# Convolution, output gate and key/value halves move beside the input projection, and half of the first output projection moves between attention steps

## The chip, the cores and the metric

The program runs on one core of a Trainium2 chip. The metric is the device time of one execution in microseconds (us), the median of several runs. Engines are named as in the profile: PE (TensorE), PEld (its weight loads), DVE (VectorE), ACT (ScalarE), POOL (GpSimd), SP (SyncE, which here only issues DMAs).

## What is computed

One layer of an encoder for 2,048 prompt tokens and 64 tokens of a running stream, all float32:

```python
gq, gk, gv, gr, glow, sq, sk, sv, cb, cc, ch = split_cols(x @ w_in)      # x is layer-normed
# A: gated linear attention, 4 heads, state carried over chunks of 64 tokens
lg = jax.nn.log_sigmoid(glow @ w_gate_up + b_gate) / GLA_TAU
S_fin, go = gla_seq(S0, gq * DK ** -0.5, gk, gv, lg)
go = go * lax.rsqrt(mean(go * go) + eps) * gla_norm_g * silu(gr)
# B: stick-breaking attention, 4 heads of 64, blocks of 128 queries, 512 cached keys for the stream
so = sb_attention(sq, k_all, v_all, past_len)
# C: short convolution of three taps over tokens
cy = conv3(cc * ch);  co = cb * cy
x = layer_norm(ALPHA * x + concatenate([go, so, co]) @ w_out)
x = layer_norm(ALPHA * x + square(relu(x @ w_up)) @ w_down)
```

The outputs are the two results, the new keys and values, the recurrent states and the last two rows of cc * ch.

## The kernel before

All matrix products of the layer are done as three passes over halves: an operand x is split into a rounded half (ACT copies it to fp32r, "hi") and a rest (DVE subtracts, "lo"), and `split_product` (L108 to L113) issues hi·hi, lo·hi, hi·lo. Three phases follow one another, each with its own buffers and a barrier at its end.

**phase_in** (L120) is the input projection. Tokens go in four groups (512, 512, 512 and 576). The columns of w_in go in six chunks of about 512; per group and chunk, PE runs four to eight units of 24 matmuls each. A written-out list `order` holds the steps norm (layer norm of one tile of 128 tokens), turn (its transposes, L357, and their halves), weights (halves of one chunk's eight row blocks) and product; every engine walks this one list. All four tiles of group 0 are normed and turned before the first product (L111 to L113). ACT evicts each unit and stores it: to `zt_scratch` transposed, to `gv_scratch`, or to the outputs of new keys and values.

**phase_gla** (L383) is the recurrence. Groups of 512 tokens, tiles of 128; again one list for all engines. For each group there is work ahead: gate, gate_log, gate_sum (decays, L701, L705), six levels of decayed products (level_arg L744 and L745, level_mul L754 and L760, level_product L859, level_put L790), and silu_exp and silu (three passes on ACT, L652 to L656, four on DVE, L732), which is spread between the steps of the tiles of the group before it. Per tile: v_in (load of values, L601), intra L903, inter L924, state L809, squares, root, turn, kv (L891) and norm (L820, L823), whose result store_tile (L566) puts into `mixt_scratch`. Beside all this POOL computes the convolution alone, in 10 pieces of at most 512 tokens (L948 to L983), from rows that phase_in stored.

**phase_tail** (L990) is attention, output projection and feed-forward. Attention is a list of 171 periods (one slot of scores z L1794 to L1796, sigmoids L1544 and L1545, scan L1671, product L1681 or on POOL L1715, turn L1808, weigh L1821 and L1822); 20 of them belong to the first 512 tokens. Keys and values are read back from the outputs in six pieces, transposed and split (pk L1782, L1522, L1642; pv; p_store L1435 and L1437 to `ks_scratch` and `vs_scratch`) and these steps stand between the first 20 periods. Then come rows, xn, mix_load (L1417), mix (halves of the eight row blocks of the mixed values: 0 to 3 from A, 4 and 5 from B, 6 and 7 from C), and the output projection: for the first group 16 steps `out` of 12 matmuls, eight on blocks 0 to 3 (kh = 0) and eight on 4 to 7 (kh = 1). Feed-forward steps up and down follow, and the other 151 periods are spread over them by `price` and `cost`, so that each group's attention is there before its output projection. SP issues all loads and stores of the tail in the same order, and a wait on SP holds back whatever stands behind it.

## Time and profile before

| | |
|---|---|
| median of 3 runs | 3114.15 us (3110.86 to 3116.0) |
| the profiled execution | 3112.73 us, of which the span is 3110.9 us |
| phase_in, to 640.9 us | first product at 42.3 us, last at 637.3 us |
| phase_gla | 640.9 to 959.7 us |
| phase_tail | from 959.7 us, first `out` at 1110.5 us |
| busy over the span | PE 88%, DVE 48%, ACT 34%, POOL 11% |
| mean granted clock of PE | 0.934 |

A busy time is the sum of an engine's instructions in a stretch; matmuls overlap, so their durations add up to more than their stretch, and what one costs in a row of them is the distance of two starts.

### The profile page before, as it was taken

The page shows a single profiled execution, that of the slowest core. Times are in us where ns is not written, and L with a number is a line of the kernel's source. Part 1 is how long each engine was busy: PE and PEld are TensorE (multiplying, and loading weights), DVE is VectorE, ACT ScalarE, POOL GpSimd, SP SyncE. Part 2 cuts the span into 40 slices and gives each one's busy share as a digit, 9 for nine tenths or more (in the row PEclk, how much of TensorE's full clock was granted, in tenths as well). Part 3 has the DMA queues.
Part 4 walks back from the last instruction along what each step waited for, and adds up shares of the span by engine and source line. Part 5 has one row for each costly group of instructions (what it writes and reads, how often), then busy time and mean ns, then how long its engine had stood idle before and what let it go on. Part 6 is the DMA issues. An engine that isn't in the chain of part 4 may idle for free. (4 is left out here: it accounts for less than half of the span.)

```text
span 3110.9 us, 38667 instructions
## 1 busy us (share of the span) xinstructions
PE 2734.4 (88%) x13838; PEld 2268.3 (73%) x13838; DVE 1505.1 (48%) x2247; ACT 1069.5 (34%) x1783; POOL 329.9 (11%) x283
## 2 busy tenths in 40 slices
PE   5999999946662467999998999999999988999997
PEld 4787789835541356888877888877888766888885
DVE  5333342158883556665656544446644425522224
ACT  3323333223342424443443444443434321322221
POOL 1100010056600000000001100001100000000000
PEclk9999999966786588999999999999999989999998
DMA  5544454233315654575655766565766554544452
GB/s 185 169 160 153 160 180 126 85 121 88 89 45 187 191 191 140 169 249 179 216 193 191 229 218 209 191 206 183 234 190 227 170 171 144 190 157 158 154 168 98
DMA packets 362107, 526.11 MB, mean 169 GB/s; under 512 B 28832, under 2 KB 208208, under 8 KB 361920
## 3 DMA queue, kind: packets, MB, share of 16 engines
q1 hardware_dynamic: 337696, 480.23, 48.1%
q10 hardware_dynamic: 18832, 26.10, 2.3%
q0 software_dynamic: 5392, 17.31, 1.6%
q8 instruction: 115, 1.88, 0.3%
q14 instruction: 72, 0.59, 0.1%
HBM read 422.74 MB, written 100.80 MB: 168 GB/s over the span
## 5 line engine op out<-in xcount | busy, mean ns | idle before, releaser
L111 PE MATMUL p_ps_u<-p_xh,p_wh 128*128 128x512 f32 (+1 forms) x1280 | 453.1, 354 | 5.4 <-DVE p_xl L1626 5.4
L112 PE MATMUL p_ps_u<-p_xh,p_wl 128*128 128x512 f32 (+1 forms) x1280 | 451.5, 353 | 0.0
L113 PE MATMUL p_ps_u<-p_xl,p_wh 128*128 128x512 f32 (+1 forms) x1280 | 451.0, 352 | 0.0
L1575 DVE SCALAR_TENSOR_TENSOR p_res<-p_res,p_ps_d 128x512 f32<-128x512 f32 (+1 forms) x340 | 232.1, 685 | 451.4 <-PE p_ps_d L113 445.7
L111 PE MATMUL p_ps_d<-p_wh,p_hh 128*128 128x512 f32 (+1 forms) x1088 | 433.2, 398 | 16.9 <-DVE p_res L1575 14.8
L112 PE MATMUL p_ps_d<-p_wh,p_hl 128*128 128x512 f32 (+1 forms) x1088 | 428.6, 394 | 0.0
L113 PE MATMUL p_ps_d<-p_wl,p_hh 128*128 128x512 f32 (+1 forms) x1088 | 428.4, 394 | 0.0
L1484 ACT ACTIVATE p_wh<-p_wst 128x1024 fp32r<-128x1024 f32 x288 | 293.9, 1049 | 276.6 <-PE p_ps_d L113 225.0
L1633 DVE TENSOR_TENSOR p_r<-p_r 128x512 f32<-128x512 f32 (+1 forms) x160 | 95.8, 599 | 461.3 <-ACT p_hh L1514 461.3
L1507 ACT ACTIVATE p_r<-p_ps_u 128x512 f32<-128x512 f32 (+1 forms) x160 | 83.8, 524 | 579.5 <-PE p_ps_u L113 579.4
L111 PEld LDWEIGHTS p_ps_u<-p_xh,p_wh 128*128 128x128 f32 x1280 | 241.2, 188 | 35.5 <-DVE p_xl L1626 6.2
L113 PEld LDWEIGHTS p_ps_u<-p_xl,p_wh 128*128 128x128 f32 x1280 | 241.2, 188 | 31.0
L112 PEld LDWEIGHTS p_ps_u<-p_xh,p_wl 128*128 128x128 f32 x1280 | 241.2, 188 | 28.3
L111 PEld LDWEIGHTS p_ps_d<-p_wh,p_hh 128*128 128x128 f32 (+1 forms) x1088 | 204.0, 187 | 66.4 <-DVE p_res L1575 19.1
L111 PE MATMUL p_ps_m<-p_xh,p_wh 128*128 128x512 f32 (+3 forms) x680 | 242.4, 356 | 1.4 <-DVE p_xl L320 1.4
L112 PE MATMUL p_ps_m<-p_xh,p_wl 128*128 128x512 f32 (+3 forms) x680 | 242.9, 357 | 0.0
L113 PE MATMUL p_ps_m<-p_xl,p_wh 128*128 128x512 f32 (+3 forms) x680 | 241.2, 355 | 0.0
L113 PEld LDWEIGHTS p_ps_d<-p_wl,p_hh 128*128 128x128 f32 (+1 forms) x1088 | 203.4, 187 | 48.3
L329 DVE TENSOR_TENSOR p_wl<-p_wst,p_wh 128x512 fp32r<-128x512 f32 (+1 forms) x192 | 127.6, 703 | 224.6 <-ACT p_wh L272 224.4
L112 PEld LDWEIGHTS p_ps_d<-p_wh,p_hl 128*128 128x128 f32 (+1 forms) x1088 | 204.1, 188 | 44.0
L1715 POOL TENSOR_TENSOR p_aw<-p_sg,p_keep 128x512 f32<-128x512 f32 (+2 forms) x84 | 89.9, 1070 | 1363.3 <-DVE p_keep L1671 1363.3
L1544 ACT ACTIVATE p_tg<-p_ps_z 128x512 f32<-128x512 f32 (+5 forms) x168 | 87.4, 520 | 323.1 <-PE p_ps_z L1796 322.9
(155 smaller groups left out, 4473.0 us busy)
## 6 DMA issues: line engine op xcount, KB each, us to landing
p_wl<-wlo_scratch SPq DMA_DIRECT2D x216, 512.0 KB, 5.1
p_wst<-in_w_up SPq DMA_DIRECT2D x128, 512.0 KB, 6.0
p_wst<-in_w_down SPq DMA_DIRECT2D x128, 512.0 KB, 4.6
wlo_scratch<-p_wl SPq DMA_DIRECT2D x72, 512.0 KB, 3.6
p_wst<-in_w_in SPq DMA_DIRECT2D x128, 256.0 KB, 3.6
p_kk<-ks_scratch SPq DMA_DIRECT2D x84, 256.0 KB, 5.9
p_vv<-vs_scratch SPq DMA_DIRECT2D x84, 256.0 KB, 4.5
p_wst<-in_w_out SPq DMA_DIRECT2D x32, 512.0 KB, 6.0
```

What stands on the lines that cost most here:

```text
L111: pe.matmul(out, lhs_hi, rhs_hi, start=first, stop=False, skip_group_check=skip)
L112: pe.matmul(out, lhs_lo, rhs_hi, start=False, stop=False, skip_group_check=skip)
L113: return pe.matmul(out, lhs_hi, rhs_lo, start=False, stop=last, skip_group_check=skip)
L329: dve.tensor_tensor(wl[:, gc % 2, k, :width], wst[:, u % WSTAGE, :width], wh[:, gc % 2, k, :width].bitcast(F32), ALU.subtract).then_inc(wl ...
L1484: act.activation(wh[:, u % WRING, :], wst[:, u % WSTG, :], ACT.Copy).then_inc(whi_done, 1)
L1507: act.activation(r[:, i % 2, :cc], ps_u[:, i % 2, :cc], ACT.Relu).then_inc(relu_done, 1)
L1544: act.activation(tg[:m, n % SIG, 512 - w:512], ps_z[:m, :w], ACT.Sigmoid, scale=-SCALE).then_inc(sig_done, 1)
L1575: dve.scalar_tensor_tensor(out=acc, in0=acc, scalar=scale, in1=ps_d[:c, d % DB, :], op0=ALU.mult, op1=ALU.add).then_inc(d_free, 1)
L1633: dve.tensor_tensor(r[:, i % 2, :cc], r[:, i % 2, :cc], r[:, i % 2, :cc], ALU.mult).then_inc(sq_done, 1)
L1715: pool.tensor_tensor(aw[:m, u % AW, i, :w], sg[:m, n % SIG, :w], keep[:m, n % KEEP, 513 - w:513], ALU.mult).then_inc(a_pool, 1)
```

## The change

In phase_in the list is written out unit by unit: a product waits only for its own tile where it can, the chunk gv comes first, weights are split three blocks per unit, and the layer norm takes its root on POOL. Units get kinds: `silu` (ACT applies a sigmoid while evicting, DVE multiplies by the value and the norm's weight), `cc`/`ch`/`cb` (DVE does the convolution and stores into `mixt_scratch`), and `kv`, whose values are split at once and whose keys are transposed (kturn) and split, straight into `ks_scratch` and `vs_scratch`. phase_gla loses silu_exp, silu and all of POOL's convolution; it loads the finished gate instead. phase_tail prepares only the cached keys and values. Blocks 6 and 7 of the mixed values are split before 4 and 5; those two are loaded after the eight `out` steps with kh = 0, and in the first group these eight steps stand between the first 20 periods.

```diff
@@ phase_in
+    chunks = [([(C_GV, 512)], "T"), ([(C_GQ, 512)], "F"), ([(C_GR, 528)], "F"), ([(C_SK, 512)], "T"), ([(C_CC, 512)], "F"),
+              ([(C_SQ, 256), (C_CB, 256)], "F")]
...
+                        order += [("norm_b", x + 1)] * (x + 1 < len(us)) + [("turn", x)]
+                    order += [("norm_a", x + 2)] * (x + 2 < len(us))
...
+                order += more[3 * x:3 * x + 3]
+                order.append(("unit", i))
+                order += late.pop(0)
...
+                if units[i]["kind"] == "kv":
+                    late[0].append(("kturn", i))
+                    late[1].append(("kstore", i))
...
+                        act.activation(slot[:u["mw"], :u["n"]], ps[:u["mw"], :u["n"]], ACT.Sigmoid if kind == "silu" else ACT.Copy).then_inc(a_out, 1)
...
+                            dve.tensor_tensor(cu[:, x, at_u + 2:at_u + 2 + n], ps[:, c:c + n], cin[:, c:c + n], ALU.mult).then_inc(d_out, 1)
...
+                            dve.tensor_scalar(y, cu[:, x, at_u + 2:at_u + 2 + n], cw[:, x, 2:3], None, ALU.mult).then_inc(conv_step, 1)
+                            for w in range(2):
...
+                                dve.scalar_tensor_tensor(out=y, in0=cu[:, x, at_u + w:at_u + w + n], scalar=cw[:, x, w:w + 1], in1=y,
+                                                         op0=ALU.mult, op1=ALU.add).then_inc(conv_step, 1)
...
+                    for p in range(2):
+                        mm = pe.transpose(ps_t[:, q, p * P:p * P + n], outb[:n, slot_no[i] % OUTS, p * P:p * P + P], ident[:n, :n])
+                    mm.then_inc(k_turned, 1)
...
+                        if i == by_chunk[gc][0]:
+                            pe.wait_ge(wlo_done, KT * gc + k + 1)
@@ phase_gla
-                if li == 0:
-                    todo.append((("silu_exp", g), 0))
-                elif li == 2:
-                    todo.append((("silu", g), 3))
...
-                    if g >= 1:
-                        sp.wait_ge(gg_done, g)
-                    sp.dma_start(gr[:, :, :n], zt_dram[Z_GR:Z_GR + 512, t0:t0 + n].rearrange("(a p) t -> p a t", p=P)).then_inc(gr_in, 16)
+                    if g >= 2:
+                        sp.wait_ge(o_gate, tiles_before[g - 1])
+                    sp.dma_start(gg[:, sl_, :, :n], zt_dram[Z_GR:Z_GR + 512, t0:t0 + n].rearrange("(a p) t -> p a t", p=P)).then_inc(gg_in[sl_], 16)
...
-            for k, (x, t, n) in enumerate(pieces):
...
-                pool.dma_start(mixt_dram[768 + cp:768 + cp + P, t:t + n], y).then_inc(c_out[sl_], 16)
@@ phase_tail
-            steps = [("mix", g, k) for k in range(KT)]
+            steps = [("mix", g, k) for k in (0, 1, 2, 3, 6, 7)]
             for kh in range(2):
+                if kh:
+                    steps += [("mix_load", g, 4), ("mix_load", g, 5), ("mix", g, 4), ("mix", g, 5)]
...
-        mixed = [i for i, st in enumerate(dense) if st[0] == "mix" and st[2] == 0]
+        mixed = [i for i, st in enumerate(dense) if st[0] == "mix_load" and st[2] == 4]
...
+        order += [("q_load", 0), ("k_load", 0), ("q_prep", 0)]
+        add_attention(1)
+        order += [("w_load", 0), ("w_load", 1), ("p_load",)]
+        add_attention(2)
+        split_weights(-1)
...
+            if i < mixed[0]:
+                if st[0] == "out":
+                    seen += 1
+                    order += prep[seen // 2 - 1:seen // 2] if seen % 2 == 0 else []
+                    add_attention(2 + (group_end[0] - 2) * seen // (firsts + 1))
+                continue
```

The lists move instructions in three places that matter below. First, SP's queue in phase_gla near the third tile of group 0: p_gr (now p_gg) is the gate, p_on a tile's result, p_v the values of the tile after next. Before:

```order
L594 DMA p_gr<-zt_scratch 128x4x512 [waits p2_gg_done]
L566 DMA mixt_scratch<-p_on 128x4x128 [waits p2_o_gate]
L601 DMA p_v<-gv_scratch 128x512 [waits p2_o_mm]
L566 DMA mixt_scratch<-p_on 128x4x128 [waits p2_o_gate]
L601 DMA p_v<-gv_scratch 128x512 [waits p2_o_mm]
```

Now:

```order
L780 DMA p_gg<-zt_scratch 128x4x512 [waits p2_o_gate]
L755 DMA mixt_scratch<-p_on 128x4x128 [waits p2_o_gate]
L787 DMA p_v<-gv_scratch 128x512 [waits p2_o_mm]
L755 DMA mixt_scratch<-p_on 128x4x128 [waits p2_o_gate]
L787 DMA p_v<-gv_scratch 128x512 [waits p2_o_mm]
```

The sequence is the same, but the first load, with a result's store and the values' load behind it, now waits for o_gate, the results of all four tiles of the group, where it waited for gg_done.

Second, PE at the start of the tail, where p_ps_z are scores, p_ps_d an `out` step and p_ps_a transposes (L1885 those of the cached keys, L1911 of weights). Before:

```order
L1782 MATMUL p_ps_a<-p_ident,p_res 128x128 x12
L1794 MATMUL p_ps_z<-p_causalb,p_identb 128x128
L1795 MATMUL p_ps_z<-p_kk,p_qh 128x128
L1796 MATMUL p_ps_z<-p_kk,p_ql 128x128
L1782 MATMUL p_ps_a<-p_ident,p_res 128x128 x4
L1794 MATMUL p_ps_z<-p_causalb,p_identb 128x128
```

Now (of each `out` step's 12 matmuls the last three stand here):

```order
L1899 MATMUL p_ps_z<-p_kk,p_ql 128x256
...
L111 MATMUL p_ps_d<-p_wh,p_xh 128x512
L112 MATMUL p_ps_d<-p_wh,p_xl 128x512
L113 MATMUL p_ps_d<-p_wl,p_xh 128x512
L1897 MATMUL p_ps_z<-p_causalb,p_identb 128x128
L1898 MATMUL p_ps_z<-p_kk,p_qh 128x128
L1899 MATMUL p_ps_z<-p_kk,p_ql 128x128
L1897 MATMUL p_ps_z<-p_causalb,p_identb 128x128
L1898 MATMUL p_ps_z<-p_kk,p_qh 128x256
L1899 MATMUL p_ps_z<-p_kk,p_ql 128x256
L1911 MATMUL p_ps_a<-p_ident,p_aw 128x128 x3
L111 MATMUL p_ps_d<-p_wh,p_xh 128x512
```

After the first two periods one `out` step stands before every two further periods.

Third, DVE's queue at the start of phase_in: L451 are weight rests, L435 and L438 the norm of a tile, L417 to L426 its statistics, L445 the rests of a turned tile. Now:

```order
L445 TENSOR_TENSOR p_xl<-p_ps_t,p_xh 128x4x128 x2
L451 TENSOR_TENSOR p_wl<-p_wst,p_wh 128x512
L454 TENSOR_SCALAR p_gn<-p_gn 128x4
L451 TENSOR_TENSOR p_wl<-p_wst,p_wh 128x512 x7
L435 SCALAR_TENSOR_TENSOR p_xn<-p_xs,p_mv,p_g_b 128x1024
L438 SCALAR_TENSOR_TENSOR p_xn<-p_xn,p_rstd,p_b_b 128x1024
...
L451 TENSOR_TENSOR p_wl<-p_wst,p_wh 128x512 x3
L435 SCALAR_TENSOR_TENSOR p_xn<-p_xs,p_mv,p_g_b 128x1024
L438 SCALAR_TENSOR_TENSOR p_xn<-p_xn,p_rstd,p_b_b 128x1024
L445 TENSOR_TENSOR p_xl<-p_ps_t,p_xh 128x4x128 x2
```

Tile 1 is turned behind tile 2's norm and three weight rests of the next chunk; before, all four tiles stood ahead of the first product.

## Rows read from the trace of the kernel before

**Rows 1.** Windows of the whole core by stage; columns are in its first row

```profile
core 0: us, PE busy (x) PEld busy (x) DVE busy (x) ACT busy (x) POOL busy (x), PEclk, DMA share, GB/s
...
42.30:637.60 595.30, 595.27 (x2960) 493.11 (x2960) 182.88 (x288) 185.90 (x340) 38.45 (x26) 1.00 0.45 146
640.90:725.90 85.00, 37.46 (x154) 28.72 (x154) 59.33 (x63) 20.86 (x19) 63.10 (x51) 0.55 0.34 114
725.90:788.90 63.00, 40.53 (x278) 31.91 (x277) 55.40 (x85) 26.93 (x32) 37.05 (x38) 0.80 0.36 93
788.90:859.40 70.50, 42.51 (x277) 34.40 (x276) 60.39 (x85) 26.93 (x32) 37.22 (x38) 0.76 0.38 98
859.40:920.00 60.60, 38.10 (x293) 31.13 (x292) 52.44 (x88) 27.80 (x36) 0.00 (x0) 0.83 0.17 43
959.70:1110.50 150.80, 47.26 (x191) 36.92 (x191) 65.27 (x101) 53.95 (x112) 9.14 (x11) 0.52 0.69 221
1110.50:1136.00 25.50, 25.46 (x113) 20.83 (x114) 11.99 (x18) 6.42 (x12) 0.64 (x1) 0.94 0.41 131
...
1230.00:3060.00 1830.00, 1773.32 (x8902) 1485.23 (x8900) 875.43 (x1262) 656.44 (x1081) 113.42 (x93) 0.99 0.59 191
```

**Rows 2.** Timeline of TensorE, first products: start us, duration us, instruction [idle before]

```profile
42.29 0.79 PE L111 MATMUL p_ps_m<-p_xh,p_wh 128*128 128x512 f32 x1 [1.41 <-DVE p_xl L320]
```

**Rows 3.** Timeline of TensorE, one tile's eight transposes in mid-projection

```profile
96.10 1.04 PE L357 MATMUL p_ps_t<-p_ident,p_xn 128*128 128x128 f32 x8
```

**Rows 4.** Groups by form, 641 to 957 us: busy us, mean ns | idle before

```profile
L760 DVE TENSOR_TENSOR p_qb<-p_ex,p_gq 64x512 f32<-64x512 f32 x48 | 42.0, 874 | 0.8
...
L732 DVE SCALAR_TENSOR_TENSOR p_gg<-p_gr,p_gn,p_gg 128x512 f32<-128x512 f32 x16 | 12.6, 846 | 0.0
```

**Rows 5.** The first of these groups from 850 to 900 us, with GpSimd idle

```profile
L760 DVE TENSOR_TENSOR p_qb<-p_ex,p_gq 64x512 f32<-64x512 f32 x9 | 6.1, 683 | 0.1
```

**Rows 6.** The same view from 671 to 716 us, GpSimd busy

```profile
L760 DVE TENSOR_TENSOR p_qb<-p_ex,p_gq 64x512 f32<-64x512 f32 x12 | 15.7, 1306 | 0.2
```

**Rows 7.** Timeline of all engines around the end of the recurrence's first group

```profile
775.55 0.50 SPq L601 DMA_DIRECT2D p_v<-gv_scratch  x1
...
785.27 0.68 PE L891 MATMUL p_ps_s<-p_v,p_kt 64*64 64x128 f32 x16
...
785.88 1.12 PE L839 MATMUL p_ps_g<-p_glow,p_wgu 16*128 16x512 f32 x2
...
786.79 1.50 DVE L823 TENSOR_TENSOR p_on<-p_on,p_gg 128x512 f32<-128x512 f32 x1
...
792.98 1.23 DVE L701 SCALAR_TENSOR_TENSOR p_gy<-p_gy,p_ga 128x1024 f32<-128x1024 f32 x1 [4.18 <-ACT p_ga L635]
```

**Rows 8.** DMA issues, 640 to 957 us: KB each, median us to landing

```profile
p_v<-gv_scratch SPq DMA_DIRECT2D x16, 256.0 KB, 3.6
```

**Rows 9.** Timeline of SP's queue at the start of the tail

```profile
959.72 0.35 SPq L1360 DMA_DIRECT2D p_ident<-in_ident  x1
...
1002.57 0.38 SPq L1378 DMA_DIRECT2D p_wst<-in_w_out  x1
...
1012.87 0.38 SPq L1378 DMA_DIRECT2D p_wst<-in_w_out  x1
...
1094.60 0.46 SPq L106 DMA_DIRECT2D p_g_b<-in_ln_g  x1
```

**Rows 10.** Timeline of TensorE, first product of the output projection and two later

```profile
1110.54 0.80 PE L111 MATMUL p_ps_d<-p_wh,p_xh 128*128 128x512 f32 x1 [19.71 <-DVE p_xl L1607]
...
1134.09 0.39 PE L111 MATMUL p_ps_d<-p_wh,p_xh 128*128 128x512 f32 x1
1134.32 0.39 PE L112 MATMUL p_ps_d<-p_wh,p_xl 128*128 128x512 f32 x1
```

**Rows 11.** Timeline of TensorE, scores of two attention steps

```profile
1083.56 0.56 PE L1795 MATMUL p_ps_z<-p_kk,p_qh 128*128 128x256 f32 x1
...
1088.66 0.71 PE L1795 MATMUL p_ps_z<-p_kk,p_qh 128*128 128x512 f32 x1
```

754 lines of the change are left out of this document (415 added, 339 removed).

## The prediction, made before the change was run

> **What bounds the kernel now.** I read the windows by stage first, for the share of each engine in each stage, then the timelines where stages begin and end, then the groups of the recurrence by form. In the windows, PE is busy for all of the 595.3 us behind the first product of phase_in, while DVE works 183 us and ACT 186 [rows 1]. So that phase is PE's, and only its first 42.3 us, in which no product runs, can be shortened [rows 2]. In phase_gla DVE leads: 59.3 of the 85 us of the work ahead, 55.4 of 63 in group 0, 60.4 of 70.5 in group 1; there POOL computes the convolution. In group 2 POOL is idle, and DVE needs 52.4 us for the same kind of group [rows 1]. In the tail, 150.8 us pass before the first `out`, and PE is busy for 47.3 of them at a mean granted clock of 0.52, which is nearly all the lower level, 1.2 GHz. From 1230 to 3060 us it is busy for 97% at 0.99, 2.4 GHz. PE's chain sets the end: time moved out of the waiting stretches is gained, work added in the full stretches is paid.
>
> **phase_in.** The first product waits for a DVE rest (its idle names p_xl) and comes at 42.29 us because four tiles are normed and turned ahead of it. Now it needs one tile. Group 0's first chunk is four units of 24 matmuls, 96 at a pitch of 0.23 us [rows 10], 22 us, plus some 2.5 for the first at half clock (0.79 against 0.39 us) [rows 2, 10]: it ended near 66.8 us. In the new list the later units of the chunk wait for DVE, which has per tile a norm, two rests and three weight rests in front: some 7.5 us, an estimate from DVE operations of 0.7 to 1.5 us of like form [rows 4, 7]. With the first product near 15 us and the fourth tile near 50, the second chunk begins at about 57: a gain of 9.8. What is added to PE: the new keys are transposed here, 34 pairs of 128 x 128 at 0.13 us each transpose (1.04 for eight) [rows 3], half of them in place of idle PE time at the start and group changes, so 34 x 0.13 = 4.4 us. The convolution, gate product, halves of values and keys lie on DVE and ACT, whose busy share of 31% covers them; if that cover failed, PE would wait at units for a PSUM buffer. Sum **-5 us**, ends 0 (each unit waits as DVE comes) and -12.
>
> **phase_gla.** Three of the four constants of the convolution and its loads no longer stand at the start: 1.5 us, taken as a tenth of the idle there. While POOL works, DVE's decayed products take 1306 ns instead of 683 [rows 5, 6]: 12 x 0.62 = 7.5 us in the work ahead. The other DVE operations of that stage I take at 4 more, an estimate from the mean of the whole phase, 874 against 683 [rows 4, 5]. In groups 0 and 1 DVE is busy 3.0 and 8.0 us longer than in group 2 [rows 1]; less the part of it that is `silu` I take 9.5. The `silu` passes themselves, 16 of 0.85 us, are 12.6 [rows 4] with 0.9 of overhead. Together -36 us.
>
> Against it stands a new wait. SP now issues the load of a group's gate only when o_gate shows that all four tiles of the group two before it have been normed and gated. Behind it stand a result's store and p_v, the values of a tile that the next group needs. Before, the p_v that group 1 starts with was issued at 775.55; the last result of group 0 was gated from 786.79, for 1.50 us [rows 7]. So p_v would be issued no sooner than about 789.2 and, with 3.6 us to land [rows 8], be there at 792.8, where kv (L891) used it at 785.27 [rows 7]: 7.6 us late. DVE, the bound of this stage, goes on meanwhile with work ahead, but the list lets it do only what stands before the tile's own steps (it idled 4.18 us at 792.98 once before, for ACT). Two crossings at 7.6 and a third, shorter one at 6 make +21 us. What is behind the wait: on SP stores and loads, on PE the state's product and all of the next tile. Between -36 (the wait is hidden, as the values of that tile are due later) and 0 (a late p_v moves the work ahead too) I take **-15 us**.
>
> **phase_tail.** The stage before the first `out` held, on SP, one pair of weight units per 10 us (1002.57, 1012.87), and the normed rows only at 1094.60; 15.9 us later came the first `out` [rows 9, 10]. In the new list two attention periods and two pairs are ahead of the rows. From the start at 959.7, 6 us for constants and two pairs at 10 bring the rows to 986, with 15.9 and one more to 1003. Only what is new relative to this start counts. Then 18 periods and eight `out` steps alternate. Two starts of scores two periods apart are 5.1 us apart [rows 11], and an `out` of 12 matmuls costs 12 x 0.23 = 2.7 us at full clock [rows 10]. PE waits within the periods, so part of it is covered: I take 7.0 us for a round of two periods and one `out`, between 5.1 and 7.8. Nine rounds are 63 us, the first `out` at half clock adds 2.7, the cached keys' preparation between them 8: 1077 us. Then the attention's result is stored, blocks 4 and 5 are loaded and split: twice 3.6 us [rows 8] and 2 of halves. kh = 1 starts near 1087. Before, it started eight `out` steps behind 1110.54, at 1135 to 1136 (113 matmuls run there in 25.5 us) [rows 1, 10]: -48 us. More attention is now left behind that point (by my count of the list, 20 periods lie before it, where 22 did), which costs some PE time in the full stretch: two to three slots of about 1.2 us, +3. In later groups blocks 4 and 5 are loaded in the middle of a group, beside dense work; one wait moves, none is added, 0 with ends at 3 either way. Sum **-45 us**, ends -22 (rounds of 9 us, one more load in line) and -60 (rounds of 5.3).
>
> The clock weighs here. The row shows 0.52 in the stretch in which PE works in pieces of one to two us between waits, and 0.94 as soon as `out` steps run without a break [rows 1]. My sum uses full clock for all but the first. The Trainium skill ("TensorE: Matmul & The Clock Gate", section "HAM oscillation — how this bites in real kernels") says that short bursts of matmuls between waits make each burst start at the lower clock again. This case's 0.52 agrees with that for attention steps; no row shows it for an `out` between them. By that rule the result would be the one of the third case below.
>
> **Sum.** -5 - 15 - 45 = -65 us. The profiled execution took 3112.73, so 3047.7; the median of the runs is 1.4 above it, so **3049 us**.
>
> **The rivals, and how the numbers follow.**
>
> *As summed*, 3049 us: 0.50.
>
> *The late values are hidden.* For: the v_in behind the gate may be of a tile whose state step comes late, and DVE has work ahead to fill with; against: kv at 785.27 stands 2 us before the end of the group. Then phase_gla gives its -36, and if the periods also run at the pace of 5.3 us a round, 31 us in all: 3018 us. 0.25.
>
> *The `out` steps between attention run at half clock.* For: 0.52 in the same stretch. Against: one `out` adds 2.7 us of dense work to each round. At half clock it costs 5.4 instead of 2.7: seven more at 2.7 us are 19: 3068 us. 0.18.
>
> *Slower than before.* The change holds the rows' order to attention: every `out` waits in PE's queue behind periods that wait for ACT and DVE, and these in turn wait behind it. In the kernel before, the 20 periods with their preparation took from 988 to about 1090, 102 us, 10.2 for two. If that pace, and not 5.1 us, is attention's own, a round costs 10.2 + 5.4 at half clock + 1 of preparation, 16.6 us, and nine of them 150. kh = 1 then starts at 1003 + 150 + 9 = 1162, 26 us later than before, and with the displaced periods the tail is 29 longer: 29 - 5 - 15 = +9, 3122 us. The mechanism decides from a round of about 15.6 us. Against: most of that pace came from loading keys (pairs of loads at 10 us), which the change removes. 0.04.
>
> *Nothing to measure.* The halved load of the convolution's stage does not shorten it and the tail's gain is lost again at the next group's end: 0.03.
>
> A measurement of this kernel can tell about 0.2%, 6 us, from no change. Faster: 0.50 + 0.25 + 0.18 = 0.93, same 0.03, slower 0.04. The range reaches below the second case by 10 us, 3008, since phase_in's end of -12 and the tail's of -60 can add to it, and above the third by 24, 3092, for phase_gla's end of 0.
>
> **What would show it.** Right: first product near 15 us and the second chunk near 57, last product of phase_in near 632 to 636; DVE's decayed products at about 690 ns throughout and POOL idle in phase_gla; phase_gla about 304 us long, with waits of kv on DMA p_v near the ends of groups; first `out` about 43 us behind the start of the tail, kh = 1 about 127 behind it; scores two periods apart at 7 us. Wrong: a DVE or ACT wait inside phase_in's units, which lets PE's busy share fall below 97%; no wait on p_v (then the second case); a granted clock of 0.5 in the alternating stretch (the third); rounds above 10 us (the fourth). I would also be wrong if attention, now two periods later, missed the end of the second group, seen as waits of PE for mix_load 4 in the later groups.

## The result, and the profile after

The changed kernel took 3084.11 us in the median of four runs (3081.57 to 3086.94), the kernel before 3113.14 in the runs beside it: a ratio of 0.9907, interval 0.9889 to 0.9924. It is faster, by 29 us where 65 were forecast. The profiled execution took 3083.57 us, its span is 3081.8.

Four points that both programs have split the span: the last product of phase_in, the first load of the tail (`p_ident`), the first product of kh = 1 of the first group, and the end. In the kernel before they lie at 637.28, 959.72, 1135.45 and 3110.9 us; two of them are these products, and its second chunk of phase_in begins at 68.23:

```profile
68.23 0.48 PE L111 MATMUL p_ps_m<-p_xh,p_wh 128*128 128x512 f32 x1
...
637.28 0.29 PE L113 MATMUL p_ps_m<-p_xl,p_wh 128*128 128x288 f32 x1
...
1135.45 0.39 PE L111 MATMUL p_ps_d<-p_wh,p_xh 128*128 128x512 f32 x1
```

| stretch | before | after | difference | forecast |
|---|---|---|---|---|
| phase_in to its last product | 637.3 | 638.3 | +1.0 | -5 |
| from there to the tail | 322.4 | 319.8 | -2.6 | -15 |
| tail to kh = 1 | 175.7 | 122.1 | -53.6 | -48 |
| kh = 1 to the end | 1975.5 | 2001.5 | +26.0 | +3 |

The windows of the changed kernel, columns as in [rows 1]:

```profile
core 0: us, PE busy (x) PEld busy (x) DVE busy (x) ACT busy (x) POOL busy (x), PEclk, DMA share, GB/s
15.60:62.30 46.70, 31.46 (x120) 24.22 (x121) 28.26 (x41) 12.59 (x23) 4.95 (x7) 0.82 0.56 181
62.30:638.60 576.30, 574.88 (x2899) 475.85 (x2897) 240.93 (x409) 179.88 (x350) 20.29 (x28) 1.00 0.48 152
642.00:708.90 66.90, 29.68 (x154) 21.79 (x154) 44.49 (x58) 15.36 (x16) 6.10 (x2) 0.67 0.25 84
708.90:779.40 70.50, 41.09 (x277) 31.96 (x276) 49.41 (x81) 21.32 (x29) 0.00 (x0) 0.77 0.20 61
779.40:851.30 71.90, 41.91 (x277) 32.55 (x276) 49.28 (x81) 21.32 (x29) 0.00 (x0) 0.78 0.20 59
851.30:917.10 65.80, 38.89 (x277) 32.45 (x276) 49.30 (x81) 20.94 (x29) 0.00 (x0) 0.81 0.13 37
958.10:1000.80 42.70, 1.53 (x7) 1.10 (x7) 9.79 (x15) 10.36 (x17) 0.76 (x2) 0.50 0.80 274
1000.80:1080.20 79.40, 50.21 (x247) 40.44 (x247) 48.70 (x75) 34.25 (x77) 8.85 (x9) 0.80 0.47 146
1005.00:1035.00 30.00, 24.23 (x133) 19.40 (x132) 25.28 (x40) 16.38 (x39) 4.21 (x5) 0.99 0.38 116
1080.20:3080.00 1999.80, 1884.42 (x9395) 1573.71 (x9395) 972.94 (x1399) 694.89 (x1153) 131.36 (x108) 0.97 0.57 183
```

In phase_in PE is busy for 31.5 of the first 46.7 us behind the first product, then it is full. The work ahead of phase_gla lasts 66.9 us instead of 85.0, and POOL has two instructions left in it and none in the groups; but groups 0, 1 and 2 last 70.5, 71.9 and 65.8 us, where [rows 1] has 63.0, 70.5 and 60.6 (one group up to 920), with DVE busy for only some 49.3 in each. In the tail the alternating stretch has full clock (0.99 from 1005 to 1035; 0.80 is the mean from the first `out` to kh = 1). The first products of each part, on PE's timeline:

```profile
15.63 0.76 PE L111 MATMUL p_ps_m<-p_wh,p_xh 128*128 128x512 f32 x1 [2.10 <-DVE p_wl L451]
...
37.51 0.79 PE L111 MATMUL p_ps_m<-p_wh,p_xh 128*128 128x512 f32 x1 [9.18 <-DVE p_xl L445]
...
1000.77 0.79 PE L111 MATMUL p_ps_d<-p_wh,p_xh 128*128 128x512 f32 x1 [34.54 <-DVE p_xl L1714]
...
1080.27 0.76 PE L111 MATMUL p_ps_d<-p_wh,p_xh 128*128 128x512 f32 x1 [9.44 <-issue]
...
1565.89 0.47 PE L111 MATMUL p_ps_d<-p_wh,p_xh 128*128 128x512 f32 x1 [2.03 <-issue]
...
2054.25 0.77 PE L111 MATMUL p_ps_d<-p_wh,p_xh 128*128 128x512 f32 x1 [7.05 <-issue]
...
2569.00 0.76 PE L111 MATMUL p_ps_d<-p_wh,p_xh 128*128 128x512 f32 x1 [7.40 <-issue]
```

37.51 is the second unit of phase_in, late by 9.18 us. The last four are the first products of kh = 1 in groups 0 to 3. Each stands behind a wait, and the kernel before has none of the four: there the products of kh = 1 followed those of kh = 0 with nothing between. ACT's timeline names what the last of them waits for, the load of blocks 4 and 5:

```profile
2566.68 1.43 ACT L1603 ACTIVATE p_xh<-p_hh 128x576 fp32r<-128x576 f32 x2 [4.82 <-DMA p_hh<-mixt_scratch]
```

DVE's decayed products take 682 ns throughout, as forecast (874 in [rows 4]):

```profile
L923 DVE TENSOR_TENSOR p_qb<-p_ex,p_gq 64x512 f32<-64x512 f32 x48 | 32.7, 682 | 0.8
```

Why the groups gain nothing by it stands on SP's queue at the end of group 0:

```profile
744.48 0.47 SPq L777 DMA_DIRECT2D p_gk<-zt_scratch  x1
765.94 0.36 SPq L780 DMA_DIRECT2D p_gg<-zt_scratch  x1
766.35 0.51 SPq L755 DMA_DIRECT2D mixt_scratch<-p_on  x1
766.90 0.50 SPq L787 DMA_DIRECT2D p_v<-gv_scratch  x1
```

and on PE's timeline there:

```profile
773.45 1.15 PE L1055 MATMUL p_ps_s<-p_v,p_kt 64*64 64x128 f32 x16 [9.66 <-DMA p_v<-gv_scratch]
774.52 2.07 PE L1003 MATMUL p_ps_g<-p_glow,p_wgu 16*128 16x512 f32 x2
...
779.43 2.08 PE L1067 MATMUL p_ps_o<-p_att,p_v 128*128 128x128 f32 x8
```

SP stands for 21 us at p_gg. The store and the load of p_v behind it go out at 766.35 and 766.90, and kv waits 9.66 us for the values. The same happens twice more, 9.53 us at 845.34 and 6.70 at 914.31.

### The profile page after: what moved, and what is told of

The parts are those of the page before. It is cut to its first block and busy times, and to the rows that moved or that the text cites. A ratio compares the mean times of both kernels' runs of the same rounds, so it can differ in the third digit from the quotient of the medians.

```text
span 3081.8 us, 38633 instructions
## 1 busy us (share of the span) xinstructions
PE 2721.1 (88%) x13838; PEld 2254.1 (73%) x13838; DVE 1521.8 (49%) x2339; ACT 1027.9 (33%) x1758; POOL 178.2 (6%) x169
## 5 line engine op out<-in xcount | busy, mean ns | idle before, releaser
L451 DVE TENSOR_TENSOR p_wl<-p_wst,p_wh 128x512 fp32r<-128x512 f32 (+1 forms) x192 | 123.9, 689 | 135.7 <-ACT p_wh L348 134.7
L111 PE MATMUL p_ps_d<-p_wh,p_xh 128*128 128x512 f32 (+1 forms) x272 | 115.2, 424 | 78.1 <-issue 43.6
```

The lines of the kernel that those rows point to most:

```text
L111: pe.matmul(out, lhs_hi, rhs_hi, start=first, stop=False, skip_group_check=skip)
L451: dve.tensor_tensor(wl[:, gc % 2, k, :width], wst[:, w % WSTAGE, :width], wh[:, gc % 2, k, :width].bitcast(F32), ALU.subtract).then_inc(wl ...
```

## The experiments

Fifteen kernels ran. Each is the changed kernel with the edit shown; none leaves out any work. "From kh = 1" means from the first product of kh = 1 of group 0 to the end of the profiled execution. One profile scatters: phase_gla takes 319.4 to 328.3 us, from the last product to the tail, in the kernels whose edit doesn't touch it, and the stretch from kh = 1 takes 2000.7 to 2004.6 in the six kernels that have the change's tail. A difference below that is not read from one profile, so the 2.6 us by which phase_gla is shorter than before are none. Steadier is the rest of phase_in behind the first product of its second chunk: 575.0 to 575.2 us wherever that part is left alone. Times are medians; the interval of a ratio is some 5 us wide to either side, so two medians 6 us apart are not told apart.

### The wait for o_gate

**g1_gate_late.** The gate's load is issued at the last tile's store:

```diff
-                    if g >= 2:
-                        sp.wait_ge(o_gate, tiles_before[g - 1])
-                    sp.dma_start(gg[:, sl_, :, :n], zt_dram[Z_GR:Z_GR + 512, t0:t0 + n].rearrange("(a p) t -> p a t", p=P)).then_inc(gg_in[sl_], 16)
+                    if g < 2:
+                        sp.dma_start(gg[:, sl_, :, :n], zt_dram[Z_GR:Z_GR + 512, t0:t0 + n].rearrange("(a p) t -> p a t", p=P)).then_inc(gg_in[sl_], 16)
...
                 elif it[0] == "norm":
                     store_tile(sp, it[1])
+                    g = tiles[it[1]][0]
+                    if it[1] == group_tiles[g][-1] and g + 2 < NG:
+                        t0, n = GG[g + 2]
+                        sp.dma_start(gg[:, g % 2, :, :n], zt_dram[Z_GR:Z_GR + 512, t0:t0 + n].rearrange("(a p) t -> p a t", p=P)).then_inc(gg_in[g % 2], 16)
```

> The changed kernel, with one move in phase_gla: the load of a group's gate into the buffer of two groups before is issued behind the store of that group's last tile, so that its wait on o_gate holds nothing back on SP. Theory (SP's wait on o_gate is what ate the gain of phase_gla): the three waits of kv on p_v (9.66, 9.53 and 6.70 us of PE's idle time) go, groups 0, 1 and 2 last about 60 us instead of 70.5, 71.9 and 65.8, and the phase shortens from 316 to 286-294 us; the time falls to 3054-3062 us. Rival (the crossings are set by the gate chain, for which DVE idles 7.7 to 8.3 us at gate_sum, and the values only come late beside it): p_v is early, but DVE idles as long at gate_sum, the phase shortens by less than 8 us, the time stays above 3075 us.

Measured: 3055.02 us, ratio 0.9816 (0.9801 to 0.9831), 29 us less than the change. PE's timeline at the same crossing:

```profile
766.07 0.68 PE L1058 MATMUL p_ps_s<-p_v,p_kt 64*64 64x128 f32 x16
766.68 1.12 PE L1006 MATMUL p_ps_g<-p_glow,p_wgu 16*128 16x512 f32 x2
...
769.69 1.90 PE L1070 MATMUL p_ps_o<-p_att,p_v 128*128 128x128 f32 x8
```

kv starts without a wait, and the next tile 3.6 us behind it instead of 6.0 (779.43 - 773.45), since the gate products between them (L1003 and L1006 of the two kernels) take 1.12 us and not 2.07: behind the wait they run at the lower clock. Groups 0 to 2 last 61.1, 61.2 and 58.0 us, the tail begins at 928.9 instead of 958.15, and from the last product of phase_in to it pass 291.0 us instead of 319.8 (289.7 to 291.7 in the three kernels below that have this edit too). The theory holds. DVE's waits for the gate's chain, of which the rival spoke, fell with it, from 40.9 to 32.5 us in all: in part they hung on the late kv.

### The start of phase_in

**i1_turn_first**

```diff
-                        order += [("norm_b", x + 1)] * (x + 1 < len(us)) + [("turn", x)]
+                        order += [("turn", x)] + [("norm_b", x + 1)] * (x + 1 < len(us))
```

> The changed kernel, but in the first chunk of phase_in a tile is turned ahead of the norm of the next one, not behind it. Theory (DVE's queue sets the start: the second unit waited 9.18 us for rests that stand behind three weight rests and the next tile's norm, some 7 us): the second unit starts near 31 instead of 37.5 us, and the second chunk 4 to 7 us earlier than 62.3; the time falls by 4 to 7 us. Rival (the arrival of weights and ACT's halves set it, for which DVE waits 0.7 to 1.9 us at each rest): the first chunk ends within 2 us of 62.3 all the same, since the later units wait for their tiles instead; no change beyond 3 us.

Measured: 3086.67 us, ratio 0.9917 (0.9897 to 0.9938); the second unit starts at 34.49, the second chunk at 62.71 (37.51 and 63.14 in the change). The rival holds. ACT's timeline names the wait:

```profile
28.39 0.63 ACT L348 ACTIVATE p_wh<-p_wst 128x512 fp32r<-128x512 f32 x1 [6.18 <-DMA p_wst<-in_w_in]
29.80 0.63 ACT L348 ACTIVATE p_wh<-p_wst 128x512 fp32r<-128x512 f32 x1 [0.78 <-DMA p_wst<-in_w_in]
31.51 0.63 ACT L348 ACTIVATE p_wh<-p_wst 128x512 fp32r<-128x512 f32 x1 [1.08 <-DMA p_wst<-in_w_in]
32.04 0.58 ACT L368 ACTIVATE p_outb<-p_ps_m 128x512 f32<-128x512 f32 x1
32.52 1.08 ACT L340 ACTIVATE p_xh<-p_ps_t 128x512 fp32r<-128x512 f32 x2
```

ACT waits for three weight loads, then evicts the first unit, and only then makes the turned tile's halves (p_xh, 32.52).

**i2_weights_later** is i1 and this, to remove that:

```diff
-                order += more[3 * x:3 * x + 3]
+                order += more[3 * x:3 * x + 3] if gc else []
                 order.append(("unit", i))
                 order += late.pop(0)
+                order += more[3 * x - 3:3 * x] if not gc and x else []
```

> The changed kernel, but in the first chunk of phase_in a tile is turned ahead of the next tile's norm, and the weights of the second chunk are split only behind the units 1, 2 and 3 (three, three, two blocks), none behind unit 0. In the run that changed the first of these alone, ACT waited 6.2 us for a weight load before each group of three halves, with the turned tile's halves behind it. Theory (ACT's and DVE's queues hold the turned tile behind weights whose loads have not landed): the second unit starts at 28 to 31 us instead of 37.5, the second chunk begins at 53 to 58 instead of 62.3 us, last product of phase_in 4 to 8 us earlier; the time falls by 4 to 8 us. Rival (the second chunk then waits for its own weights, which come one in 1.3 to 2 us): the second chunk's first unit stalls between its row blocks for what was gained, and the last product stays within 2 us of 638.6.

Measured: 3092.85 us, ratio 0.9937 (0.9922 to 0.9951), 9 us worse than the change, last product at 644.08. The second unit does start at 28.78, but the next two start at 39.82 and 51.56, and the second chunk at 66.98:

```profile
34.65 0.60 ACT L369 ACTIVATE p_outb<-p_ps_m 128x512 f32<-128x512 f32 x1 [6.91 <-PE p_ps_m L113]
...
35.14 1.14 ACT L349 ACTIVATE p_wh<-p_wst 128x512 fp32r<-128x512 f32 x2
37.21 0.63 ACT L349 ACTIVATE p_wh<-p_wst 128x512 fp32r<-128x512 f32 x1 [0.93 <-DMA p_wst<-in_w_in]
37.74 1.07 ACT L341 ACTIVATE p_xh<-p_ps_t 128x512 fp32r<-128x512 f32 x2
```

Behind a unit ACT now has its eviction (waited for 6.91 us), the weights and the next tile in a row, so that units no longer overlap with the halves of the next. The theory fell, and the rival's last product within 2 us of 638.6 did too.

**i3_norms_first** restores the old start:

```diff
-        order = [("x_load", 0), ("consts",), ("x_load", 1), ("norm_a", 0), ("norm_b", 0), ("norm_a", 1), ("turn", 0)]
-        order += [("w", 0, k) for k in range(KT)] + [("x_load", 2), ("norm_b", 1), ("x_load", 3)]
+        order = [("x_load", 0), ("consts",), ("x_load", 1), ("norm_a", 0), ("norm_b", 0), ("norm_a", 1)]
+        order += [("w", 0, k) for k in range(KT)] + [("norm_b", 1), ("turn", 0), ("x_load", 2), ("norm_a", 2), ("norm_b", 2), ("turn", 1)]
+        order += [("x_load", 3), ("norm_a", 3), ("norm_b", 3), ("turn", 2), ("turn", 3)]
...
-                    if x:
-                        order += [("norm_b", x + 1)] * (x + 1 < len(us)) + [("turn", x)]
-                    order += [("norm_a", x + 2)] * (x + 2 < len(us))
```

> The changed kernel, but in phase_in all four tiles of the first group are normed and turned ahead of the first product, as in the kernel before (units, kinds and everything behind the first chunk are those of the change). This undoes the start alone. Theory (the new start ends the first chunk at 62.3 instead of some 67 us, a gain of 5, and no more, since ACT waits for weights' loads with the turned tile's halves behind them): first product at 38 to 43 us, the second chunk from 64 to 68 us, last product of phase_in 2 to 6 us later than 638.3; time 3086-3090 us. Rival (the new start is worth the 9.8 us that were forecast, and something else in the phase took 5 of them): last product 8 us or more later, 3092 us or above.

Measured: 3085.0 us, ratio 0.9917 (0.9897 to 0.9936): no difference (its profiled execution is the longest, 3094.73, with the longest phase_gla of all). PE's timeline:

```profile
38.42 0.78 PE L111 MATMUL p_ps_m<-p_wh,p_xh 128*128 128x512 f32 x1
...
62.38 0.48 PE L111 MATMUL p_ps_m<-p_xh,p_wh 128*128 128x512 f32 x1
```

First product 22.8 us later than in the change, second chunk 0.8 us earlier, last product 637.46. Both expectations missed: the interleaved start is worth nothing. The 5 us that the first chunk ends earlier than before come from the rest of the start, which both have (first product at 38.42 with the old order, 42.29 before; which of its parts does it was not tried).

**i4_kturn_twice** does PE's transposes of new keys twice:

```diff
-                    for p in range(2):
+                    for p in (0, 1, 0, 1):
```

> The changed kernel, but PE does each transpose of new keys twice, into the same place (34 transposes of 128 x 128 more, no other engine does more). Theory (PE bounds phase_in behind the first product, and a transpose costs it its full 0.13 us): last product of phase_in 4 to 5 us later, time 3087-3090 us. Rival (they fall into PE's gaps, and the 5.9 us that the phase is longer behind its first chunk are something else): last product within 1 us of 638.3.

Measured: 3088.7 us, ratio 0.9929 (0.9912 to 0.9945), last product at 641.56. The phase behind the first chunk takes 578.1 us instead of 575.2: 2.9 us for 34 transposes more, 0.09 each. They are on the path. The 0.13 of the forecast was the duration of eight by eight; eight in a row hold the next product back by 0.79 us (67.44 to 68.23 in the kernel before), 0.10 each. One pair in the change:

```profile
137.74 0.38 PE L567 MATMUL p_ps_t<-p_ident,p_outb 128*128 128x128 f32 x2
137.88 0.48 PE L111 MATMUL p_ps_m<-p_xh,p_wh 128*128 128x512 f32 x1
138.19 0.39 PE L112 MATMUL p_ps_m<-p_xh,p_wl 128*128 128x512 f32 x1
```

From the pair's start to the product behind it pass 0.14 us (0.36 with the pair done twice), and from that product to the next 0.31 instead of 0.23, in both kernels. So a pair costs 0.22 us, of which doubling shows only the part of the transposes, and 17 pairs cost 3.7. Behind its first chunk the phase is 6.1 us longer than before (638.31 - 63.14 against 637.28 - 68.23). Besides the pairs, three transposes of new tiles wait for DVE's norm, 1.4 us in all, where none did before; the last us is open.

### The tail up to kh = 1

**u1_attention_first** takes the first group's attention out from between the `out` steps, and issues the load of blocks 4 and 5, in every group, ahead of the last of those with kh = 0 (in groups 1 to 3 this is the edit of m2 below):

```diff
             elif st[0] == "mix":
+                if st == ("mix", 0, 0):
+                    add_attention(group_end[0])
...
+                    order += prep[seen:seen + 1]
                     seen += 1
-                    order += prep[seen // 2 - 1:seen // 2] if seen % 2 == 0 else []
-                    add_attention(2 + (group_end[0] - 2) * seen // (firsts + 1))
...
                 if kh:
-                    steps += [("mix_load", g, 4), ("mix_load", g, 5), ("mix", g, 4), ("mix", g, 5)]
+                    steps += [("mix", g, 4), ("mix", g, 5)]
                 for h in range(2):
+                    if h and not kh:
+                        steps += [("mix_load", g, 4), ("mix_load", g, 5)]
```

> The changed kernel, but the first group's attention is not spread between its out steps: all 20 periods stand ahead of the first halves of the mixed values, the eight out steps of kh = 0 follow in one row with the cached keys' preparation between them, and blocks 4 and 5 are loaded ahead of the last four out steps in every group. Theory (the gain of the tail up to kh = 1 came from spreading: the out steps fill PE's waits for ACT and DVE): without it kh = 1 starts 10 to 20 us later than at 1080.3, the time is 3090-3100 us. Rival (it came from what is no longer done there, the preparation of new keys and the convolution's blocks, and from the earlier load of rows; PE's time is not what bounds this stretch): kh = 1 starts within 5 us of 1080.3 or earlier, the time is 3075-3086 us.

Measured: 3078.45 us, ratio 0.9894 (0.9878 to 0.9911), 6 us less than the change, as m2 alone (3078.37).

```profile
1050.99 0.79 PE L111 MATMUL p_ps_d<-p_wh,p_xh 128*128 128x512 f32 x1 [5.05 <-DVE p_xl L1717]
...
1078.63 0.75 PE L111 MATMUL p_ps_d<-p_wh,p_xh 128*128 128x512 f32 x1 [2.03 <-issue]
```

The first `out` comes 50 us later than in the change, kh = 1 1.6 us earlier, and the tail itself begins 1.9 earlier (956.28): from its start to kh = 1 pass 122.4 us, against 122.1. The rival holds: the 54 us do not come from spreading. One reserve: the early load shortens the wait ahead of kh = 1 from 9.44 to 2.03 us here, so up to 7 us of spreading's worth may hide in it. By exclusion the rest comes from what both orders share: no new keys and values are loaded, transposed and split there, and the rows are normed early. This is argued, not shown; it was not divided further.

**t1_periods_first** does six more periods in the wait for the mixed values:

```diff
+                if st == ("mix", 0, 0):
+                    add_attention(8)
-                    add_attention(2 + (group_end[0] - 2) * seen // (firsts + 1))
+                    add_attention(8 + (group_end[0] - 8) * seen // (firsts + 1))
```

> The changed kernel, but six more attention periods of the first group (eight instead of two) stand ahead of the first halves of the mixed values, in the 34.5 us in which PE waits for rows and mixed values; the other twelve are spread over the eight out steps as before. Nothing else moves: the same 20 periods precede kh = 1. Theory (between 964 and 1001 us PE only waits for loads, and each period moved there gives back the 2.5 to 3 us it takes beside the out steps): the first out comes at most 5 us later, kh = 1 starts 10 to 18 us earlier than 122 us behind the start of the tail, and the whole gain reaches the end: 3066-3075 us. Rival (the wait is not PE's alone: the loads of keys and values put ahead hold back rows and weights on SP, and ACT and DVE make the halves later by what the periods take): the first out comes 10 us or more later, and the time stays within 4 us of 3084.

Measured: 3082.58 us, ratio 0.9903 (0.9888 to 0.9918). First `out` 12.8 us later, kh = 1 7.0 us earlier (1073.24), and the stretch from there 2008.9 us, 7.4 longer than in the change: what was won ahead of kh = 1 was lost behind it, and nothing is clear in the time. ACT shows what the periods waited for:

```profile
1001.23 0.42 ACT L1643 ACTIVATE p_qh<-p_qraw 128x256 fp32r<-128x256 f32 x1 [17.92 <-DMA p_qraw<-zt_scratch]
```

The third head's queries came 17.9 us late: they stand on SP behind rows and mixed values, were issued from 990.16, and the slowest load of queries took 10.3 us to land where the median took 3.0. The window 958 to 1000.8 above has 274 GB/s and a DMA share of 0.80, and t1 from 958.7 to 1001.2 has 297 and 0.88. The opening of the tail is a stretch of loads, and PE's 34.5 us of idle are no free room.

**t2_periods_more** is t1 with four periods of the second group ahead of kh = 1, two of them behind the load of blocks 4 and 5 (its diff is against t1):

```diff
-        begun, spent = group_end[0], 0.0
+        begun, spent = group_end[0] + 4, 0.0
...
+                if st == ("mix_load", 0, 5):
+                    add_attention(group_end[0] + 4)
...
-                    add_attention(8 + (group_end[0] - 8) * seen // (firsts + 1))
+                    add_attention(8 + (group_end[0] + 2 - 8) * seen // (firsts + 1))
```

> As the run with eight periods first, and four periods of the second group are done ahead of kh = 1 too, two of them over the load of blocks 4 and 5. Theory (part of what the tail gave back is attention displaced into the full stretch: a period costs about 2.5 us there, PE's passes for it and the clock and waits around it, and next to nothing in a wait): kh = 1 starts 2 to 6 us later than with the eight periods alone, the stretch behind it is 9 to 12 us shorter, the time is 4 to 9 us below that run's. Rival (the stretch behind kh = 1 is not shortened by fewer periods, since its end is set by waits at the group changes): the time is that of the other run or a few us above it.

Measured: 3100.83 us, ratio 0.9958 (0.9941 to 0.9975), 18 us worse than with eight periods alone. kh = 1 starts at 1100.84, 27.6 us later, of which 4.8 lie ahead of the tail; from kh = 1 it takes 2003.0 us, 5.9 less than t1 where 9 to 12 were expected, and no less than the change. The theory fell: four periods cost over 20 us here and give back 6 at most.

### From kh = 1 to the end

**m1_mix_first** puts blocks 4 and 5 of groups 1 to 3 ahead of the first `out`, as before the change:

```diff
-                if kh:
+                if kh == (0 if g else 1):
                     steps += [("mix_load", g, 4), ("mix_load", g, 5), ("mix", g, 4), ("mix", g, 5)]
```

> The changed kernel, but in groups 1 to 3 blocks 4 and 5 are loaded and split ahead of the first out step, as in the kernel before; group 0 keeps the new order. Theory (the tail gave back 27 of its 54 us mostly by a new wait ahead of kh = 1 in each later group: 2.03, 7.05 and 7.40 us of idle and some 2 us of lower clock behind each of the two long ones): these waits go, the waits ahead of the first out step stay at 5 to 7 us as in the kernel before, and the time falls by 15 to 22 us to 3062-3069. Rival (the time was given back by attention that was displaced from the first group into the full stretch): the time stays within 5 us of 3084 and the wait turns up ahead of the first out step instead.

Measured: 3081.48 us, ratio 0.9901 (0.9886 to 0.9916), from kh = 1 1999.9 us. The waits ahead of kh = 1 are gone in these groups, but in the first group's feed-forward six scores waited for q rests, 11.2 us together, where one did in the kernel before (1.9) and three in the change (5.7). This is one of them:

```profile
1493.29 0.29 PE L1897 MATMUL p_ps_z<-p_causalb,p_identb 128*128 128x128 bf16 x1 [2.60 <-DVE p_ql L1760]
```

**m2_mix_early** issues only the two loads earlier in these groups, ahead of the last `out` steps of kh = 0:

```diff
-                    steps += [("mix_load", g, 4), ("mix_load", g, 5), ("mix", g, 4), ("mix", g, 5)]
+                    steps += [] if g else [("mix_load", g, 4), ("mix_load", g, 5)]
+                    steps += [("mix", g, 4), ("mix", g, 5)]
                 for h in range(2):
+                    if g and h and not kh:
+                        steps += [("mix_load", g, 4), ("mix_load", g, 5)]
```

> The changed kernel, but in groups 1 to 3 the two loads of blocks 4 and 5 are issued ahead of the last four or five out steps of kh = 0 and split behind them, so that 11 us of products lie over the load. Theory (the wait ahead of kh = 1 is the round trip of load and halves with nothing in its place): no idle over 1.5 us ahead of kh = 1 in any of these groups, 3062-3070 us, about as fast as with both blocks first. Rival (attention of the group is late, and the loads wait for its result): the wait moves with the load, the idle ahead of kh = 1 stays at 5 us or more and the time falls by less than 6 us.

Measured: 3078.37 us, ratio 0.9887 (0.9865 to 0.9909), from kh = 1 1997.4 us. The waits ahead of kh = 1 shrink to 2.0 to 2.2 us, 10 us less together; the time hardly follows. Both theories of a single cause had failed by here.

**m3_old_plan** is m1 and the counts of attention periods of the kernel before:

```diff
+        first_out = [i for i, st in enumerate(dense) if st[0] == "out"][0]
-        price = [0.0 if i in quiet or i < mixed[0] or i >= mixed[-1] else cost.get(st[0], 0.0) * (st[1] if st[0] == "pause" else 1) for i, st in enumerate(dense)]
+        price = [0.0 if i in quiet or i < first_out or i >= mixed[-1] else cost.get(st[0], 0.0) * (st[1] if st[0] == "pause" else 1) for i, st in enumerate(dense)]
...
                     add_attention(2 + (group_end[0] - 2) * seen // (firsts + 1))
+                spent += price[i]
                 continue
```

> The changed kernel with blocks 4 and 5 ahead of the first out step in groups 1 to 3, and with the attention of everything behind kh = 1 of the first group planned as in the kernel before: 22 periods precede that point instead of 20 (the last two over the load of blocks 4 and 5), and the counts of periods in front of each up, down and out step behind it are those of before. Theory (what the tail gave back was the order of the later groups: waits ahead of kh = 1, and, in the run that only moved the two blocks, attention planned at other places, whose q rests came 2.2 to 2.6 us late six times): from kh = 1 to the end it takes 1976 to 1985 us, as before (1975.5), instead of 2001.5; kh = 1 itself starts 3 to 7 us later than at 1080.3; time 3060-3070 us. Rival (the give-back lies in something the change does to the later groups whatever their order, such as a lower clock or longer waits behind an earlier start): from kh = 1 to the end 1995 us or more, time 3080 us or above.

Measured: 3067.05 us, ratio 0.9848 (0.9833 to 0.9862), 17 us less than the change. The theory holds. **m4_plan_only** has this diff without that of m1.

> The changed kernel with only the plan of the run m3_old_plan: 22 periods ahead of kh = 1 of the first group and the counts of before behind it, but blocks 4 and 5 of groups 1 to 3 still loaded and split ahead of kh = 1, as the change has them. Theory (two causes of like size: the waits of 2.0, 7.1 and 7.4 us ahead of kh = 1 with the lower clock behind the two long ones, and the places of the periods): the three waits stay, from kh = 1 to the end it takes 1987 to 1995 us, time 3073-3080 us. Rival (the plan is all of it): from kh = 1 to the end 1976 to 1984 us, time 3063-3070 us. Other rival (only both together give anything): 1998 us or more, 3082-3088 us.

Measured: 3085.45 us, ratio 0.9914 (0.9901 to 0.9928): the second rival. The stretch from kh = 1 in m3, m1 and m4:

```profile
1085.30:3061.90 1976.60, 1879.88 (x9381) 1570.58 (x9381) 970.32 (x1395) 693.99 (x1148) 131.78 (x107) 0.97 0.57 185
```

```profile
1080.80:3080.70 1999.90, 1889.43 (x9395) 1578.61 (x9395) 972.17 (x1399) 694.39 (x1153) 132.17 (x108) 0.97 0.56 183
```

```profile
1082.60:3080.60 1998.00, 1886.10 (x9381) 1574.84 (x9381) 969.85 (x1395) 693.66 (x1148) 131.89 (x107) 0.97 0.56 183
```

1976.6 us with both edits, 1999.9 and 1998.0 with one of them, 2001.5 with none, 1975.5 before. PE has the same work (m3 and m4 the same count of products); in m3 it is busy 6 to 10 us less and idle 14 to 15 us less.

Two more starts on PE's timelines divide this stretch, the first `out` of group 1 and the first product of kh = 1 of group 3:

| us | kh = 1 of group 0 to `out` of group 1 | to kh = 1 of group 3 | to the end |
|---|---|---|---|
| before | 452.8 | 1011.4 | 511.2 |
| the change and the five others with its tail | 457.4 to 459.8 | 1028.6 to 1032.9 | 512.4 to 512.8 |
| m1, blocks first | 466.6 | 1022.1 | 511.2 |
| m2, loads early | 452.6 | 1031.8 | 513.0 |
| m4, old plan | 453.1 | 1032.1 | 512.7 |
| m3, both | 453.0 | 1012.4 | 511.2 |

So 20 of the 26 us lie in the middle. There m2 takes 10 us out of the waits and gains nothing, the old plan alone gains nothing, blocks first alone gains 9, and both 19. What m1 gains there it loses in the first group's feed-forward, where its waits for q rests are; the few us of m2 lie in that first part too.

### Together

**c1_gate_and_mix** is g1 with m2, **c3_gate_and_first** g1 with u1, **c2_gate_and_plan** g1 with m3.

> Two edits that were run alone are put together: the gate's load behind the last store of its group (29 us faster than the change alone) and the loads of blocks 4 and 5 ahead of the last out steps of kh = 0 in groups 1 to 3 (6 us faster). Theory (they lie in different phases and add): 3045-3053 us. Rival (the second was within the spread of the runs): 3053-3059 us.

> The gate's load behind the last store of its group, together with all 20 attention periods ahead of the first out steps and blocks 4 and 5 loaded early in every group. The two alone were 29 and 6 us faster than the change. Theory (they add): 3046-3052 us, the time of the gate's edit with blocks 4 and 5 early. Rival (the second was within the spread of the runs): 3053-3059 us.

> The gate's load behind the last store of its group, together with the plan of the run m3_old_plan. Theory (two causes in two phases, which add up to what the forecast missed): 3030-3042 us. Rival (the plan gives nothing): 3052-3060 us, the time of the gate's edit alone.

Measured: 3050.71, 3050.16 and 3031.24 us; ratios 0.9800 (0.9785 to 0.9815), 0.9791 (0.9775 to 0.9807) and 0.9736 (0.9720 to 0.9751). c2 is 53 us faster than the change and 81 faster than the kernel before (of its own runs). Its stretch from kh = 1 takes 1976.9 us, as m3's does, and 29 and 17 us alone are 46, and 53 together is not beyond the intervals of 5 us on each. By stages they agree better: phase_gla takes 289.7 us (291.0 in g1), the stretch from kh = 1 1976.9 (1976.6 in m3). The two causes add. c1 and c3 are 4 to 5 us below g1 (3055.02) and fell in the range of their theory, but their intervals overlap with g1's, so whether the second edit adds anything is not shown by them.

## Why the forecast was wrong

The forecast was of the right sign and its range (3008 to 3092) held the result. The size was missed by 36 us: more than half of the gain that was forecast did not come. The sum of stages shows where.

- **phase_in, -5: measured +1.** "The second chunk begins at about 57" failed: it began at 63.14, 6.1 later, which is a gain of 5.1 us instead of 9.8, since the kernel before began its second chunk at 68.23 and not near 66.8. The estimate of 7.5 us per tile counted DVE's work; the loads of the next chunk's weights and ACT's order were left out, and the second unit started 21.9 us behind the first, the third and fourth 10.9 and 8.3 us apart. The run with the old start shows that there was nothing to gain by the interleaving at all. Behind the first chunk 6.1 us were added where 4.4 were forecast. The transposes (there are 34, not 34 pairs; I had halved the pairs for idle PE time) are 3.7 of them with the product that each pair delays, and the waits for DVE's norm 1.4.
- **phase_gla, removed work, -36: nearly.** With the wait on SP out of the way the phase takes 291.0 us from the last product to the tail where it took 322.4, a gain of 31.4. DVE's decayed products take 682 ns, as forecast.
- **phase_gla, the new wait, +21: right in kind, too small.** It measured 29. I took the load of p_v at its usual 3.6 us [rows 8]; behind the gate's 1 MB and a store it needed 6.5 until kv began (766.90 to 773.45) and 6.4 at the second crossing. At the third the gate is 128 KB, and it needed 3.6 (910.72 to 914.31). At half clock the products behind the wait took 2.4 us more at the first two crossings and 1.0 at the third. So -36 and +21 became -31 and +29, and -15 became -3. The case in which the late values are hidden is refuted. (Its 3018 us held a slip: 21 us from the hidden wait and 15 from nine rounds of 5.3 instead of 7 are 36, not 31.)
- **Tail up to kh = 1, -48: measured -54, for another reason than I gave.** The first `out` came 42.6 us behind the start of the tail (43 forecast), the periods and `out` steps took 70 us (74), blocks 4 and 5 needed 9.4 (about 9). So the parts agree, in part by luck: one round took 14.6 us and the last, from its `out` to the wait for blocks 4 and 5, 18 us with a wait of 7.1 in it, while the other rounds were shorter than the 7.0 forecast. And I charged the gain to rounds of attention and `out`; with no rounds it is the same, up to the 7 us of the early load. The third case, half clock in that stretch, is refuted by the row from 1005 to 1035 at 0.99: PE was busy for 24 of 30 us and stood still for 1.4 at most. Where it did stand for 6.6 us, ahead of 1040.82, the next scores took 0.67 us instead of 0.42, and behind 7.1 us, at 1065.68, 0.77 instead of 0.48. The rule I had weighed (the Trainium skill, "TensorE: Matmul & The Clock Gate", section "HAM oscillation — how this bites in real kernels", bursts between waits start at the lower clock) agrees with what stands behind these waits; between the eight `out` steps there was one of them. The slower case fell with the pace: from one `out` to the next it took 4.5 to 6.8 us, once 14.6, where its bound was 15.6 each time.
- **Later groups, "one wait moves, none is added", 0 to 3: the step that failed most, +26.** The stretch took 2001.5 us against 1975.5. Waits of 2.03, 7.05 and 7.40 us are new ahead of kh = 1, and behind each of the two long ones products run at half clock (0.77 against 0.39 us), 4.5 us more by the distances of their starts: 21 of the 26 us by count. In the list kh = 0 was followed at once by the loads that kh = 1 needs; I had seen this for the first group and priced it there, and not for the others. But these waits are not the cause alone: m2 shortens these waits by 10 us, and the stretch that holds them does not get shorter. The other part is the plan: the change counts the first group's periods apart, and every later one falls at another place among dense steps. My 3 us for displaced periods priced their number and not their places. Both have to be undone before the time comes back (17 us in the median, 25 in the stretch). That each hides what the other costs is shown, and that 19 of it lie in groups 1 to 3; which engine couples them is not shown and stays open. In m1 the waits for q rests on DVE are the visible part.

## What to carry to other kernels

A wait added to an in-order DMA queue costs what stands behind it: look for the same load at a place in the queue where its condition is already true. Time won ahead of a saturated stretch has to be followed to the end, stretch by stretch between points both programs have, since here half of it was lost again behind the place of the gain. And when undoing one suspect gives nothing, undo two: edits worth 3 and 0 us alone, neither clear of noise, were worth 17 together.

## What the runs showed of the hardware

A load of 256 KB that lands in 3.4 us in the median was used 6.5 us after its issue when a load of 1 MB and a store of 256 KB stood within 1 us ahead of it, and 3.6 us after it when that load was 128 KB. A pair of 128 x 128 transposes set between products took 0.14 us and delayed the product after next by 0.08 more, 0.22 a pair; eight in a row held the next product back by 0.79, though their duration reads 1.04. In the 43 us that open the tail the queues moved 274 GB/s; with six periods more ahead of it (297 GB/s) a load of queries that usually landed in 3.0 us took 10.3, and ACT stood 17.9 us for it: idle time of PE there was not room for more work.
